# The product that sums the modulation's rows moves from behind the fifth to behind the seventh product of a down step

## What is computed

```
def swiglu_ffn(x, w_gu, w_down):
    gate, up = jnp.split(x @ w_gu, 2, axis=-1)
    return (jax.nn.silu(gate) * up) @ w_down
```

```
c_act = jax.nn.silu(c)
for layer in range(DEPTH):
    mod = jnp.einsum('bd,dn->bn', c_act, w_ada[layer]) + b_ada[layer]
    sh1, sc1, gt1, sh2, sc2, gt2 = [m[:, None, :] for m in jnp.split(mod, 6, axis=-1)]
```

## Time and profile before

| | |
|---|---|
| median of three runs | 2592.42 us |
| the profiled execution, its own time | 2591.23 us |
| its span (first to last instruction) | 2589.4 us |
| TensorE busy (PE) | 2524.0 us, 97% |
| VectorE busy (DVE) | 1391.5 us, 54% |
| ScalarE busy (ACT) | 446.8 us, 17% |
| GpSimd busy (POOL) | 193.6 us, 7% |
| mean granted TensorE clock | 0.993 of full speed |

### The profile page before, as it was taken

The page is one execution under the profiler, slowest core; times in us unless marked ns, Lnnn a source line. Parts: engine busy times, 40 slices in busy tenths (PEclk is TensorE's granted clock), DMA queues, the critical chain, the costliest instruction groups (busy, mean ns, idle before and its releaser), DMA issues.

```text
span 2589.4 us, 44358 instructions
## 1 busy us (share of the span) xinstructions
PE 2524.0 (97%) x18090; PEld 1636.1 (63%) x18090; DVE 1391.5 (54%) x2940; ACT 446.8 (17%) x1218; POOL 193.6 (7%) x316
## 2 busy tenths in 40 slices
PE   8999999999999999999999999999999999999996
PEld 7964457697499444477964659945556445645462
DVE  6788554688877866647886656664730000001102
ACT  1200252110012013221101331102311100101010
POOL 4010100001100103000011100001100000000000
PEclk9999999999999999999999999999989999999999
DMA  9684423466656734235675424454569999999997
GB/s 298 215 300 145 172 98 130 142 220 250 219 195 220 268 128 165 81 114 193 214 252 148 134 98 153 173 163 116 190 256 357 418 417 417 417 418 414 414 416 309
DMA packets 296332, 611.58 MB, mean 236 GB/s; under 512 B 15804, under 2 KB 172640, under 8 KB 287808
## 3 DMA queue, kind: packets, MB, share of 16 engines
q1 hardware_dynamic: 279024, 550.80, 57.5%
q0 software_dynamic: 17104, 57.91, 6.8%
HBM read 605.11 MB, written 3.54 MB: 235 GB/s over the span
## 4 chain that ended last, share of the span: by engine, by line
PE 83%; DVE 8%; DMA 4%; issue 3%; ACT 1%; POOL 0%; DVEq 0%; SPq 0%; POOLq 0%; ACTq 0%
PE psum L1407 23%; PE psum L1564 15%; PE psum L1990 6%; PE psum L1608 6%; PE psum L1460 4%; PE psum L1301 4%; PE psum L1700 4%; PE psum L1255 4%; DMA xn<-in_w_ada 3%; PE psum L1353 2%; PE psum L1901 2%; PE psum L2016 2%; DVE proj L3134 1%; PE psum L1599 1%; PE psum L1523 1%
## 5 line engine op out<-in xcount | busy, mean ns | idle before, releaser
L3770 DVE SCALAR_TENSOR_TENSOR proj<-proj,psum 128x256 f32<-128x256 f32 (+1 forms) x63 | 24.9, 395 | 526.6 <-ACT proj L2495 526.6
L1407 PE MATMUL psum<-xT,ring 128*128 128x128 f32 x1600 | 195.0, 275 | 0.0
L1564 PE MATMUL psum<-ring,xT 128*32 128x512 f32 (+3 forms) x2112 | 193.3, 514 | 1.6 <-DMA ring<-in_w_exp_up 1.6
L1407 PEld LDWEIGHTS psum<-xT,ring 128*128 128x128 f32 x1600 | 187.6, 192 | 5.7 <-issue 5.7
L1990 PE MATMUL psum<-ring,xT 128*128 128x384 f32 (+1 forms) x448 | 159.2, 505 | 2.1 <-ACT xT L2318 2.1
L1564 PEld LDWEIGHTS psum<-ring,xT 128*32 128x32 f32 x2112 | 78.1, 110 | 104.2 <-issue 92.9
L3134 DVE SCALAR_TENSOR_TENSOR proj<-xn,cols,proj 128x512 f32<-128x512 f32 x168 | 126.0, 750 | 18.6 <-DMA xn<-in_w_ada 14.5
L1700 PE MATMUL psum<-ring,memT 128*128 128x512 f32 x256 | 119.9, 607 | 2.5 <-issue 2.4
L1990 PEld LDWEIGHTS psum<-ring,xT 128*128 128x128 f32 x448 | 83.1, 193 | 60.2 <-issue 15.5
L1039 POOL DMA_DIRECT2D xn<-in_w_ada x96 | 69.4, 725 | 672.6 <-DVE proj L3134 665.9
L1460 PE MATMUL psum<-ring,sp_rows 128*128 128x512 f32 x220 | 105.2, 592 | 0.0
(11 more groups left out here) (601 smaller groups left out, 4222.5 us busy)
## 6 DMA issues: line engine op xcount, KB each, us to landing
ring<-in_ffn_w_gu SPq DMA_DIRECT2D x80, 1024.0 KB, 7.3
xn<-in_w_ada POOLq DMA_DIRECT2D x96, 512.0 KB, 4.8
ring<-in_ffn_w_down SPq DMA_DIRECT2D x44, 1024.0 KB, 7.0
ring<-in_w_exp_down SPq DMA_DIRECT2D x39, 1024.0 KB, 16.5
ring<-in_w_exp_gate SPq DMA_DIRECT2D x63, 512.0 KB, 12.1
ring<-in_w_exp_up SPq DMA_DIRECT2D x63, 512.0 KB, 15.2
ring<-in_xa_w_kv SPq DMA_DIRECT2D x16, 1024.0 KB, 10.2
ring<-in_w_in SPq DMA_DIRECT2D x60, 256.0 KB, 3.8
```

The lines of the kernel that those rows point to most:

```text
L1407: ins = mm(banks[bank][:, t * P:(t + 1) * P], weights(t)[:, k, :], tokens[:, k, :], start=(new and t == 0 and k == 0), stop=(k == 3), skip ...
L1564: ins = mm(o[:, :, o0:o1], xg[e % 2][:, k, 32 * g:32 * g + 32], w_[:, :, c0:c1], start=(k == 0 and n_ == 0), stop=(k == KT - 1), skip_grou ...
```

## The change

In the loop over down steps 0 to 8 on TensorE, `through_last_bank` is called behind the loop over the seven products and not inside it behind "P3". The waits, the operands, the bank and VectorE's program are as before.

```
@@ -1492,8 +1492,7 @@
                         down(d, name)
                         if d == 0 and name == "P2":
                             products(NSTEP - 1, "M4")
-                        if name == "P3":
-                            through_last_bank(NSTEP + d, 0)
+                    through_last_bank(NSTEP + d, 0)
                 for name in DOWN_PRODUCTS:
                     down(NSTEP - 2, name)
                     down(NSTEP - 1, name)
```

## The result

The changed kernel took 2603.91 us in the median of six runs (2601.37 to 2604.82), the kernel before 2593.07 (2588.98 to 2596.7). That is 10.8 us where 4.5 were forecast, and above the range (2602.0). Three single executions in the whole record ran at a far longer time (3270 to 9803 us), and no median, mean or ratio here counts them. The profiled execution has a span of 2601.9 us, 12.5 more than before.

What follows compares the result with a forecast made beforehand. VectorE's slot chain was taken to bound the down halves. A 1.72 us delay gave 3.44 us in the first and third, 0.7 in the second and 0.4 in the fourth: 4.5 us on 2592.42, so 2596.9; range 2590.3 to 2602.0.

Steps and rivals of the forecast that it cites:

- What bounds the kernel: Down half: TensorE is mostly busy, but VectorE sets its end through the stream of slots, starting at step 1's product.
- The wait in turn 1: VectorE's wait for the product of step 1 grows from 1.15 to 2.87 us in all four feed-forwards.
- The product of step 8: First feed-forward: TensorE still waits for VectorE's sum, the product ends where step 9 begins today; nothing gained or lost.
- the sign named for it: Trace sign: line 1431's wait for VectorE is still there in step 8 of the first and third feed-forward.
- P6 in step 6 of the second: Second feed-forward: P6's wait for VectorE's sums in step 6 grows from 0.66 to 2.38 us.
- I take the durations as they are: Slot transfers issued 1.72 us later keep their durations, as some move into ring-load batches and others out.
- D: Rival, chance 0.12: transfers collide more, one more 7.6 us slot per feed-forward; 8.4 us loss, 2600.8, up to 12.3.
- The slack in the second and fourth: 1.28 us of idle time in `rows_out` absorbs part of VectorE's delay; these feed-forwards lose 0.7 and 0.4 us.
- the sign named for the turning of x: Trace sign: line 1198 in the first and third comes about 1.7 us later after the start of step 0.
- B: Rival, chance 0.14: slots land when the queue allows, so waits for transfers absorb the delay; 2590.3 us.
- C: Rival, chance 0.04: TensorE's 5.9 us of waits at the moved product go and nothing replaces them; 2586.5 us.

Runs made afterwards that it cites:

- e1: Kernel before with only the product of down step 1 moved behind P4, the other three left behind P3: 1.0047 of the kernel before, 2600.97 against 2591.18 us.
- e2: Kernel before with only the products of steps 3, 6 and 8 moved behind P4, step 1 left behind P3: 1.0007 of the kernel before.
- e5: Changed kernel with a second sum buffer, VectorE using slots 12 and 13 before reading step 1's product: 0.9979 of the kernel before, 2585.68 against 2591.10 us.
- the repeat: The changed kernel run again as it is: 1.0044 of the kernel before, 2603.86 us.
- e13: Kernel before with ring loads of down weights cut to a quarter in the four feed-forwards with the modulation: 0.9996 of the kernel before, 2588.85 us.
- e14: Changed kernel with the ring loads of down weights cut to a quarter in the same four feed-forwards: 1.0024 of the kernel before, 2595.95 us.
- e3: Kernel before with the product of step 1 moved earlier, behind P2, the others behind P3: 0.9990 of the kernel before, 2588.53 against 2591.18 us.
- e9: Kernel before with only the product of step 1 moved, one place later behind P7: 1.0020 of the kernel before, 2597.36 against 2591.93 us.

## Why the prediction was wrong

**What bounds the kernel: right.** The half's end is set by VectorE's chain, which begins with the product of step 1. e1 and e2 put the whole loss on that one product, and e5 removes it by cutting that link. The chain of waits of the changed kernel in the fourth feed-forward shows it with its new length (start, us, what), against the earlier trace rows:

```profile
1341.20 0.87 PE psum L1431 x2
1342.10 0.70 DVE diff_o L3153
...
1347.09 0.76 DVE proj L3133
1348.14 7.76 DMA xn<-in_w_ada
1356.00 0.76 DVE proj L3133
```

**The wait in turn 1: right**, 2.86 us four times for 2.87.

**The product of step 8: right for the first feed-forward**, 0.89 us of wait left and step 9 within 0.5 us of its old place against step 0 (61.1 us behind it, 61.6 before). In the third the wait grew to 2.81 us. In the repeat's profile the first has no such wait and the third 2.06 us, so the sign named for it holds in one profile of two.

**P6 in step 6 of the second: right in number, partly by luck**, 2.17 us for 2.38. Counted from step 0, VectorE was 2.5 us late there and not 1.72, and TensorE, which the forecast holds level up to step 6, was 1.0 us late itself, having waited 0.77 us in step 3. The two errors nearly cancel.

**The step that failed** is the sentence "I take the durations as they are, since a shift moves some slots into such batches and others out of them": the term for longer transfers was put at nothing. The chain's waits for transfers grew from 14.5 to 19.5 us, and in the repeat to 19.1, and that growth of 5.0 us is about what the four halves lost beyond the forecast (9.2 for 4.5). Of it, 4.4 us arise in turn 2. Issued 1.72 us later, slot 14 stood farther behind the ring load before it and became faster (4.0 us for 5.0 to 5.7 in the first three feed-forwards), but slot 15 came closer to the next ring load, or beside it, and became slower in all but the first: in the second and third feed-forward VectorE waits 1.97 and 2.11 us for slot 15, which it did not wait for before, and in the fourth 3.37 us, where before no wait for a slot was over 0.9 us. With short ring loads these waits did not grow (e13, e14). The two streams keep the beat of the same loop, a down step of about 6 us, so a shift against each other need not average out over steps. How much it costs in one feed-forward varies from profile to profile: slot 15 of the first took 4.6 us in one and 7.6 in the repeat. I had the price of such a neighbour in the earlier trace rows, 4.0 against 7.6 us, and gave it the outer case D, with one slot per feed-forward and in the first and third alone. (The 4.0 us are not quite the best of these slots: the shortest of all 96 took 3.8.)

The Trainium skill ("DMA: Bandwidth & Descriptors", Queues, rings and completion order) says that a DMA engine takes turns between queues that have work. The trace fits this, in the fourth feed-forward: slot 14, issued 1.5 us ahead of the ring load, took 4.2 us, and slot 15, issued together with it, 7.8. The turns themselves no run shows. I had put this rule at the long end of the range; it belonged in the forecast.

**The slack in the second and fourth: right in size, wrong in effect.** The 1.28 us in `rows_out` were used up, but by a lateness of 3 us and more there, so these two lost 2.0 and 2.4 us where I had 0.7 and 0.4. The third lost 3.7 where I had 1.7; the first 1.2 in one profile and 3.1 in the repeat. The sum of the four is much the same in both profiles (9.2 and 9.9), the parts are not. So the sign named for the turning of x, about 1.7 us later in the first and third, failed too: it was 1.2 and 3.7 us.

**The rivals.** B, waits for transfers that absorb the delay, happened only in a part: slot 14 of the first feed-forward has now no wait (1.06 us before), and slot 15 one of 0.18 us. C is refuted by e2 as well: even the three late products alone win nothing in the runs. D, more collisions, is nearest, but its slots are not one per feed-forward, and the second and fourth did not hide them.

## What to carry to other kernels

Before moving work on an engine that looks free to wait, ask who stands still for its result today: a product that nothing delays can be the first link of another engine's chain. Where that chain issues transfers by use, a shift moves them against every other periodic transfer, and 1.7 us can become 3; price the neighbour as the forecast and not as the outer case. And look at the reader's order first: here the cure was to let VectorE do the next slots before it reads, which takes a second sum buffer (5.4 us won), after which TensorE's order no longer mattered.

## What the runs showed of the hardware

The granted clock falls in the changed kernel at places where it did not before. Two stretches of it (TensorE busy and the others, then the granted clock, DMA share, GB/s):

```profile
230.00:234.00 4.00, 2.87 (x11) 1.85 (x12) 3.50 (x11) 0.94 (x4) 0.00 (x0) 0.83 0.99 381
904.50:910.00 5.50, 5.44 (x9) 2.41 (x10) 5.50 (x15) 0.60 (x1) 0.00 (x0) 0.69 0.33 126
```

The first lies behind the waits of 0.65 and 1.49 us for x at the end of the first feed-forward, and the eight records of line 1301 that start at 232.29 take 5.37 us in place of 3.67. The second lies behind the wait of 2.81 us. So for a time TensorE runs at the lower of its two levels, 1.2 and not 2.4 GHz, and each such fall costs about 1.7 us of its work. Behind the wait of 2.17 us (666.94) it did not fall. The length of the wait alone does not decide it, nor is the place fixed: in the repeat's profile it fell at 184.0, behind a wait of 1.95 us, and did not fall behind one of 2.06 us at 902.25. Over all runs the mean granted clock was 0.9904 in the changed kernel (11 runs) and 0.9922 in the kernel before (90 runs). But where VectorE sets the end, as in the four down halves of the changed kernel, TensorE's slower work is hidden, and only falls outside them count, as the first does; the books of the halves come out without the clock. (In e1, e3 and e9 TensorE sets the end of some halves, and there a fall counts.) What share of the 10.8 us is the clock's stays open: in the two profiles, 12.5 - 9.2 = 3.3 us lie outside the halves, 1.7 of them between the first and the second, where the first fall is, and in the repeat's profile (span 2598.0) there is no such excess.
